# Two gaps in SBUF that move the high parts of the weights from 96 bytes past a multiple of 128 onto one

## What is computed

```python
def first_block(x, ...):
    # layer 0: RWKV-7 + latent attention, w_out; swiglu FFN of width 2816
    # layer 1: forgetting attention + block attention, w_out;
    #          mixture of 8 experts, top 2, each a swiglu of width 3584
    return rmsnorm(h, final_norm)

def moe_swiglu(t, router, w_gate, w_up, w_down):
    ...
    for e in range(N_EXPERTS):
        out = out + combine[:, e:e + 1] * swiglu(t, w_gate[e], w_up[e], w_down[e])

def second_block(x, ...):
    for l in range(2):        # dilated attention, RG-LRU and stick-breaking attention in one layer
        h = hybrid_layer(h, ...)   # x @ w_in (1024 x 3584), three mixers, y @ w_out (1024 x 1024)
    return rms_norm(h, final_gain)
```

## Time and profile before

| | us |
|---|---|
| median of 3 runs | 1859.04 (1858.51 to 1859.48) |
| profiled execution, its own time | 1857.7 |
| its span | 1855.9 |
| PE busy | 1805.4 (97%) |
| DVE busy | 1410.5 (76%) |
| ACT busy | 1140.9 (61%) |
| POOL busy | 96.1 (5%) |

### The profile page before, as it was taken

The page is one execution under the profiler, slowest core; times in us unless marked ns, Lnnn a source line. Parts: engine busy times, 40 slices in busy tenths (PEclk is TensorE's granted clock), DMA queues, the critical chain, the costliest instruction groups (busy, mean ns, idle before and its releaser), DMA issues.

```text
span 1855.9 us, 28476 instructions
## 1 busy us (share of the span) xinstructions
PE 1805.4 (97%) x11353; PEld 1566.4 (84%) x11353; DVE 1410.5 (76%) x1579; ACT 1140.9 (61%) x1254; POOL 96.1 (5%) x117
## 2 busy tenths in 40 slices
PE   8989999999998999999999999999999999899997
PEld 8868999988887888888888888888888887889997
DVE  6766665563637889889898888898888887886674
ACT  6544533344436767677676676776766775765753
POOL 0042000010210000000000000000000000201010
PEclk9999999998998999999999999999999999999999
DMA  8100455543316989899898898998988988533431
GB/s 357 69 24 3 179 185 182 182 159 114 114 46 273 363 341 365 328 376 356 338 369 352 342 365 340 359 358 337 373 345 343 376 355 305 181 136 137 159 137 46
DMA packets 64210, 467.17 MB, mean 252 GB/s; under 512 B 7248, under 2 KB 7376, under 8 KB 7888
## 3 DMA queue, kind: packets, MB, share of 16 engines
q1 hardware_dynamic: 64080, 465.36, 64.5%
HBM read 464.28 MB, written 1.05 MB: 251 GB/s over the span
## 4 chain that ended last, share of the span: by engine, by line
PE 86%; DVE 7%; ACT 3%; DMA 2%; issue 2%; POOL 0%; SPq 0%; ACTq 0%; DVEq 0%; POOLq 0%
PE bank L573 84%; PE bank L583 2%; DMA weight_ring<-w_dram 2%; DVE split_ring L2211 1%; ACT arena L1601 1%; ACT split_ring L1601 0%; ACT late_high L1601 0%; DVE arena L2247 0%; ACT operand_high L1601 0%; DVE arena L2216 0%; DVE operand_low L2257 0%; DVE arena L2248 0%; ACT L1601 0%; POOL squares L3083 0%; DVE arena L2981 0%
## 5 line engine op out<-in xcount | busy, mean ns | idle before, releaser
L2827 DVE TENSOR_TENSOR moe_pair_low<-weight_ring,moe_pair_high 128x2048 fp32r<-128x2048 f32 x225 | 507.1, 2286 | 14.2 <-ACT moe_pair_high L1601 13.7
L1601 ACT ACTIVATE moe_pair_high<-weight_ring 128x2048 fp32r<-128x2048 f32 x225 | 427.1, 1918 | 36.8 <-DMA weight_ring<-w_dram 35.5
L573 PE MATMUL bank<-moe_pair_high,operand_high 128*128 128x512 f32 x896 | 354.5, 396 | 2.2 <-DVE operand_low L2834 2.2
L573 PE MATMUL bank<-moe_pair_high,operand_low 128*128 128x512 f32 x896 | 352.4, 393 | 0.0
L573 PE MATMUL bank<-operand_high,split_ring 128*128 128x256 f32 x1536 | 293.4, 286 | 3.2 <-ACT split_ring L1601 1.1
L1601 ACT ACTIVATE arena<-bank 128x256 f32<-128x256 f32 (+4 forms) x221 | 88.8, 423 | 300.8 <-PE bank L573 276.5
L573 PEld LDWEIGHTS bank<-operand_high,split_ring 128*128 128x128 f32 x1536 | 240.6, 192 | 7.3 <-issue 5.1
L573 PE MATMUL bank<-moe_pair_low,operand_high 128*128 128x512 f32 x896 | 223.4, 391 | 0.0
L573 PEld LDWEIGHTS bank<-moe_pair_high,operand_high 128*128 128x128 f32 x896 | 169.0, 189 | 39.4 <-issue 2.4
L573 PEld LDWEIGHTS bank<-moe_pair_high,operand_low 128*128 128x128 f32 x896 | 169.0, 189 | 36.5
L573 PEld LDWEIGHTS bank<-moe_pair_low,operand_high 128*128 128x128 f32 x896 | 168.1, 188 | 37.4
(11 more groups left out here) (315 smaller groups left out, 3061.4 us busy)
## 6 DMA issues: line engine op xcount, KB each, us to landing
weight_ring<-w_dram SPq DMA_DIRECT2D x381, 1024.0 KB, 6.9
arena<-w_dram SPq DMA_DIRECT2D x55, 1024.0 KB, 4.8
parameters<-param_dram SPq DMA_DIRECT2D x1, 2896.5 KB, 24.5
constants<-const_dram SPq DMA_DIRECT2D x1, 2836.0 KB, 17.6
hT<-x_dram SPq DMA_DIRECT2D x1, 1024.0 KB, 5.1
out_dram<-squares SPq DMA_DIRECT2D x4, 256.0 KB, 2.2
constants<-const_dram SPq DMA_DIRECT2D x1, 128.0 KB, 4.7
parameters<-param_dram SPq DMA_DIRECT2D x1, 54.5 KB, 4.7
```

The costliest lines, as they stand in the source:

```text
L573: return pe.matmul(out, lhsT, rhs, start=start, stop=stop, skip_group_check=True)
L1601: return act.activation(out, in_, f, **kw)
L2827: tt(low_, raw_, high_.bitcast(F32), ALU.subtract).then_inc(moe_split, 1)
```

## The change

It adds two unused tensors and widens two others. No instruction is added, removed or moved: each engine has the same instructions in the same order, with other addresses.

```diff
+        sb("gap_ahead_of_parameters", 24)
         with ExitStack() as over:
-            over.enter_context(nc.sbuf_tensor("parameters_start", [P, par_at["wa2"][0]], F32))
+            over.enter_context(nc.sbuf_tensor("parameters_start", [P, P], F32))
             late_high = [over.enter_context(nc.sbuf_tensor(f"late_high{i}", [P, SLOT], F32R)) for i in range(2)]
         with ExitStack() as over:
-            over.enter_context(nc.sbuf_tensor("parameters_first", [P, par_at["wa2"][0]], F32))
+            over.enter_context(nc.sbuf_tensor("parameters_first", [P, P], F32))
             pair_high1 = over.enter_context(nc.sbuf_tensor("moe_pair_high1", [P, 2 * SLOT], F32R))
-        assert par_at["wa2"][0] + 2 * SLOT <= par_at["foxbf"][0]
+        assert par_at["wa2"][0] <= P and P + 2 * SLOT <= par_at["foxbf"][0]
         par = sb("parameters", param_dram.shape[1])
         tiny = sb("tiny", 192)
         zero16 = sb("zero16", P, BF16)
         passes_i = sb("expert_passes", 1, I32)
+        sb("gap_ahead_of_arena", 8)
```

## The result

| | before | changed |
|---|---|---|
| median of 11 runs each, us | 1859.04 (1855.54 to 1860.20) | 1865.16 (1859.75 to 1868.09) |
| profiled execution, its own time | 1857.7 | 1859.75 |
| its span | 1855.9 | 1858.0 |

The account below looks back on a forecast made before the run. PE was taken as the bound, so addresses matter by how fast it takes operands. From the profiled 1857.7 us, -8.7 + 3.3 = -5.4 gave 1852.3, and 1.3 for the median gave 1853.6 us; range 1849.5 to 1860.0.

Parts of the forecast that it names:

- The bound: Whole kernel: PE is busy for 97% of the span, and the chain that ended last is PE for 86%.
- The conversions of slots: ACT's and DVE's conversions: taken as 0 us on the path, with each to stay within 15 ns.
- Odd expert steps, 8.7 us less: 56 odd expert steps, high parts 96 bytes past a multiple of 128: aligning them saves 0.155 us each.
- The slow low parts of odd steps: Odd expert steps: 8 aligned low parts take 1.85 against 1.82 us, an after-effect that goes with the uneven stream.
- Weights in `late_high`, 3.3 us more: FFN and projections: aligned weights load more slowly, 1.2 us plus 2.3 us, of which waits hide some.
- The arena, 0: Arena buffers: they move by 128 bytes and stay at a multiple of 128, so no cost was counted.
- 128 bytes are the measure: Matmul streams: 512 columns take 226.7 ns and 256 take 120.0, the columns plus one 128-byte piece of 13.33 ns.
- The third: Rival, experts: the moved arena gets out of step modulo 256, +6.4 us in sum, 1865.4 us, slower; chance 0.10.
- The first rival: Whole kernel: the address does nothing, odd steps are slow for other reasons, time stays 1859.0 us; chance 0.12.
- The second rival: Only the experts change; the place of weights in late_high costs nothing, so 1850.3 us; chance 0.09.
- the stretches of 24: Late output projections: 24 matmuls with 16 on late_high go from 2.83 to 2.88 us; staying at 2.83 favours the second rival.
- The last rival, half of the gain: Odd expert steps: unevenness has a second cause, 4.4 us less and 3.3 more, 1857.9 us; chance 0.05.

Follow-up runs that it names:

- the pair alone: Against the kernel before, only moe_pair_high1 moved, beginning 152 columns behind the parameters' start instead of 109; 1851.73 us, ratio 0.9962.

## Why the prediction was wrong

**The bound** was right: the chain is PE's for 84 to 86% in all 14 profiles, and over the stretch of the experts it is idle for 0.01 us before and 0.04 us after. The conversions of slots stayed within 15 ns but for one group (DVE's where the high part lies in the ring, 2324 ns for 2301), and the DMA moved 252 and 251 GB/s.

**Odd expert steps, 8.7 us less.** That the place of the pair makes them slow was right, and the size was off: with the pair alone moved it gave 6.5 us in the experts and 7.0 in the medians, since `down` took a little longer. The slow low parts of odd steps were an after-effect, as taken: 1.82 us in the kernel with the pair alone, 1.81 in the changed one.

**Weights in `late_high`, 3.3 us more.** The rhythm went to 2.88 us per 24, as forecast. The price on the path is 1 to 2 us, less than the 3.3 forecast: 1.0 to 1.1 in the FFN by the traces, 1.5 in all by the estimate at equal clock, while the medians alone don't tell it from 0. In the changed kernel itself the arena's move gave part of it back (FFN 168.19, since the down slots went from 5.76 to 5.70).

**The arena, 0.** This is the step that failed: "The arena moves by 128 bytes and stays a multiple of 128." Moved alone it costs 8.9 us in the experts and 7.9 in the medians (1866.60 against 1858.7). Behind it stands the sentence that "128 bytes are the measure". The agreement of 226.7 and 120.0 ns with multiples of 13.33 ns was taken as evidence for a period of 128, but it was found on buffers that all lay at the same place modulo 256. It couldn't tell 128 from 256, and no row before could. Nor did the pattern give the size: two rows of 256 columns with one more piece each would be 2 x 13.33 = 26.7 ns per matmul, and rows 5 show 8 (0.13 us over 16); and by the same count weights at byte 96 should load more slowly, where rows 7 and 8 have them quicker.

**The rivals.** The third, that the arena gets out of step modulo 256, is what happened, at 0.10; its 1865.4 us stands beside a median of 1865.16. The agreement is partly luck. It took 3.1 more in the experts and 3.3 in the weights. The 3.1 were put on the odd `down`, "whose high part lies in the arena"; but so do the hidden values that it is multiplied with, and the one that got out of step is the even `down`, at 0.05 us for its 12 matmuls (3.0 us over 56). The traces show 4.4 in the experts, and of the medians' 6.1 that leaves 1.7 for all else, where two single profiles don't tell much (FFN 168.19 for 167.77, behind the experts 286.28 for 286.15). The parts aren't additive: the arena alone costs 8.9 and the pair alone brings 6.5, which leaves 2.4, while both together left 4.4, because the odd steps' streams now begin uneven behind a `down` out of step (3.68 us for 3.62).

The first rival, that the address does nothing, is refuted by one buffer moved by 160 bytes: 0.9962. The Trainium skill gives SBUF lines of 16 bytes ("SBUF — State Buffer", Specifications (TRN2)). 160 is a multiple of 16, so the number of lines is the same in both places and can't be what differs here. The second rival, that only the experts change, is out as well: the stretches of 24 went to 2.88 us when `late_high` alone moved. It leaned on the page "TensorE: Matmul & The Clock Gate" of the Trainium skill (Step-by-step), by which loading weights takes nothing from the running matmul. The traces don't agree: the same 16 matmuls take 1.81 to 1.92 us by where the weights lie. The last rival, half of the gain, fits no better than the forecast: three quarters of it came with the pair alone (6.5 of 8.7).

## What to carry to other kernels

When PE is the bound, compare the starts of its matmuls between buffers that differ only in address, and note each buffer's byte offset against that of the other operand, modulo 256, not its own alignment. A gap that aligns one buffer moves all behind it, so list every pair that is multiplied, both operands of each, and keep the gaps' sum a multiple of 256, or move the one buffer alone. A regularity that holds for buffers of one residue says nothing about the period. All of this was seen with float32r operands, 512 or 256 streamed columns and a weight load for each matmul; other types weren't run.

## What the runs showed that was not expected

- Addresses alone moved this kernel between 1849.03 and 1866.60 us, with the same number and sizes of matmuls.
- For streamed rows of 1024 bytes the period is 256 bytes: a move of the arena by 128 costs 8.9 us in the experts, one by 256 costs 0.3 (979.2 against 978.9), one of everything by 128 costs 0.3 (979.1 against 978.8). For weights that are loaded, 128 bytes off differs from 0 (1.90 and 1.92 us for 16), so their period isn't 128; that it is 256 wasn't tried.
- The best place depends on the roles. Streamed rows of 1024 bytes want to be in step with the weights (3.63 us for 16, 3.68 to 3.75 elsewhere). Weights of 512 bytes a partition, loaded behind 256 streamed columns, want to be 192 bytes past them (1.82 us for 16, 1.92 in step).
- The unevenness outlasts its cause: 8 aligned matmuls behind a stream out of step took 1.85 us for 1.82, and in the changed kernel the 16 matmuls behind a `down` out of step regained their rhythm in their second half.
